# Sum of the routed experts: four gathered rows on TensorE and four on VectorE, LayerNorm's weight and bias on POOL

## The reference, cut to what is needed

```
def layer_norm(x, w, b):
    mu = jnp.mean(xf, -1, keepdims=True)
    var = jnp.mean(jnp.square(xf - mu), -1, keepdims=True)
    return ((xf - mu) * lax.rsqrt(var + EPS) * w + b)

# moe_ffn: acc[token] += (expert(token) @ w2[e]) * gate     for the 8 experts of the token
# shared = (silu(tf @ sw1) * (tf @ sw3)) @ sw2;  return acc + shared
f_all = moe_ffn(...)
h = layer_norm(DEEPNORM_ALPHA * h + mod[5] * f_all, ln_w[l, 1], ln_b[l, 1])
```

## Time and profile before

| | us |
|---|---|
| median of 3 runs | 2299.19 |
| lowest and highest | 2291.56, 2300.64 |
| the profiled execution | 2297.83 |
| its span | 2296.0 |
| TensorE busy | 1926.3 (84%) |
| VectorE busy | 854.0 (37%) |
| POOL busy | 652.5 (28%) |
| ScalarE busy | 261.1 (11%) |

### The profile page before, as it was taken

The page is one execution under the profiler, slowest core; times in us unless marked ns, Lnnn a source line. Parts: engine busy times, 40 slices in busy tenths (PEclk is TensorE's granted clock), DMA queues, the critical chain, the costliest instruction groups (busy, mean ns, idle before and its releaser), DMA issues. The chain is left out here.

```text
span 2296.0 us, 31832 instructions
## 1 busy us (share of the span) xinstructions
PE 1926.3 (84%) x10720; PEld 995.3 (43%) x10721; DVE 854.0 (37%) x1780; ACT 261.1 (11%) x541; POOL 652.5 (28%) x947
## 2 busy tenths in 40 slices
PE   6999994478789979999997878597779888877894
PEld 2334442344645544555553343244455444433442
DVE  0224446854533322333332736543343222222224
ACT  2122223211100000000001110011100000000001
POOL 0000000000156645666663000000046544444440
PEclk8999997789799999999998979798789999999998
DMA  8565510020759999989993761312199999999934
GB/s 347 205 239 205 193 37 1 1 97 0 298 210 409 411 415 413 397 320 406 389 411 116 311 249 55 130 53 97 67 368 408 412 413 413 413 412 411 409 139 201
DMA packets 99830, 601.66 MB, mean 262 GB/s; under 512 B 23232, under 2 KB 23339, under 8 KB 40300
## 3 DMA queue, kind: packets, MB, share of 16 engines
q1 hardware_dynamic: 64540, 499.67, 53.7%
q0 software_dynamic: 35216, 100.98, 11.7%
HBM read 590.50 MB, written 51.92 MB: 280 GB/s over the span
## 5 line engine op out<-in xcount | busy, mean ns | idle before, releaser
L1682 PE MATMUL bank<-moe_w,blk_xT 128*64 128x256 f32 x5632 | 684.5, 398 | 3.0 <-DVE blk_xT L1758 3.0
L1682 PEld LDWEIGHTS bank<-moe_w,blk_xT 128*64 128x64 f32 x5632 | 406.7, 143 | 223.8 <-issue 38.2
L1693 PE MATMUL bank<-moe_w,xt 128*64 128x512 f32 x1408 | 332.1, 592 | 1.5 <-DVE xt L1770 1.5
L1609 POOL DMA_INDIRECT ada_rows<-v_tokens,blk_gidx x264 | 271.7, 1029 | 140.3 <-issue 135.2
L1758 DVE STREAM_TRANSPOSE blk_xT<-ada_rows 128x512 f32<-128x512 f32 x132 | 94.0, 712 | 456.3 <-PE bank L1682 433.0
L435 PE MATMUL bank<-w_in_ring,xt 128*128 128x512 f32 x544 | 246.2, 610 | 12.6 <-DMA w_in_ring<-in_odd_w_in 9.8
L1625 POOL DMA_INDIRECT y_rows<-xt,blk_sidx x176 | 179.4, 1019 | 96.9 <-issue 48.5
L1777 DVE COPY xt<-bank 128x512 f32<-128x512 f32 x176 | 121.6, 691 | 149.3 <-PE bank L1693 149.3
L1741 ACT ACTIVATE xt<-bank 128x128 f32<-128x128 f32 x174 | 48.3, 278 | 1059.8 <-PE bank L1682 1059.8
L435 PEld LDWEIGHTS bank<-w_in_ring,xt 128*128 128x128 f32 x544 | 104.1, 195 | 148.4 <-issue 137.3
L1693 PEld LDWEIGHTS bank<-moe_w,xt 128*64 128x64 f32 x1408 | 100.9, 137 | 127.5 <-issue 100.5
(11 more groups left out here) (391 smaller groups left out, 1660.7 us busy)
## 6 DMA issues: line engine op xcount, KB each, us to landing
moe_w<-in_experts SPq DMA_DIRECT2D x128, 3072.0 KB, 32.2
even_late<-in_ada_w POOLq DMA_DIRECT2D x20, 2048.0 KB, 8.1
moe_w<-y_rows SPq DMA_DIRECT2D x24, 1024.0 KB, 20.5
w_in_ring<-in_even_w_in SPq DMA_DIRECT2D x8, 2048.0 KB, 9.0
w_in_ring<-in_odd_w_in SPq DMA_DIRECT2D x7, 2048.0 KB, 13.9
ada_ring<-in_ada_w SPq DMA_DIRECT2D x4, 2048.0 KB, 7.7
ada_rows<-v_tokens,blk_gidx POOLq DMA_INDIRECT x264
w_out<-in_even_w_out SPq DMA_DIRECT2D x1, 4096.0 KB, 12.9
```

The costliest lines, as they stand in the source:

```text
L1609: pool.indirect_dma_start(came[q][:, u], None, v_quarters, bass.IndirectOffsetOnAxis(ap=gidx[q][:, u:u + 1], axis=0), bounds_check=4 * n_t ...
L1682: last = nc.tensor.matmul(g.bank[1][64 * h:64 * h + 64, 0:HID], xT[:, k], w[:, s, (2 * k + h) * HID:(2 * k + h + 1) * HID], start=k == 0, ...
L1693: last = nc.tensor.matmul(g.bank[3][64 * h:64 * h + 64, :], hT[:, 64 * m:64 * m + 64], w[:, s, at:at + 512], start=m == 0, stop=m == 1)
```

## The change

`BY_PE` goes from 5 to 4, so rows 0 to 3 are TensorE's and rows 4 to 7 VectorE's. Each transfer of two rows then has one reader. `finish` leaves VectorE: the two operations are issued by POOL, with the semaphores `ln_weighted` between them and `ln_finished` behind them. Since `z` has two halves, VectorE waits before gathering tile n (n >= 2) until POOL has finished tile n - 2. And VectorE's `scale` of tile n comes directly behind its gathering, with no `finish` between them. In the mLSTM norm the scratch `sq` becomes the first half of `g.mod_row`'s first row, which holds nothing at that time.

```diff
--- before.py
+++ after.py
@@ -520,7 +520,7 @@
 
         self.e, self.y = sb("mlstm_e", [P, 2, NT, T]), sb("mlstm_y", [P, 2, NT, P])
         self.sm, self.negsel = sb("mlstm_small", [P, 2, 3, NT]), sb("negsel", [HEADS, HEADS, P])
-        self.sq, self.st, self.w = sb("mlstm_sq", [P, NT, P]), sb("mlstm_st", [P, 2, NT]), g.ada_rows[:, 0]
+        self.sq, self.st, self.w = g.mod_row[:, 0, 0:512].rearrange("p (n c) -> p n c", n=NT), sb("mlstm_st", [P, 2, NT]), g.ada_rows[:, 0]
         self.side_loaded, self.scored, self.rows_made, self.clamped, self.exped, self.weighted, self.read, self.summed = (new_sem(g, x) for x in (
             "mlstm_w_loaded", "scores_ready", "max_rows_ready", "clamped", "exp_ready", "weights_ready", "values_used", "values_summed"))
         self.mstep, self.var_ready, self.rooted, self.normed, self.mix_turned, self.mix_copied = (new_sem(g, x) for x in (
@@ -774,8 +774,8 @@
         link(nc.vector.tensor_reduce(st[:, 0], y, AX.X, ALU.add))
         link(nc.vector.tensor_scalar(st[:, 0], st[:, 0], 1.0 / P, None, ALU.mult))
         link(nc.vector.tensor_tensor(y, y, st[:, 0].unsqueeze(2).broadcast_to([P, NT, P]), ALU.subtract))
-        link(nc.vector.tensor_tensor(self.sq[:], y, y, ALU.mult))
-        link(nc.vector.tensor_reduce(st[:, 1], self.sq[:], AX.X, ALU.add))
+        link(nc.vector.tensor_tensor(self.sq, y, y, ALU.mult))
+        link(nc.vector.tensor_reduce(st[:, 1], self.sq, AX.X, ALU.add))
         nc.vector.tensor_scalar(st[:, 1], st[:, 1], 1.0 / P, EPS, ALU.mult, ALU.add).then_inc(self.var_ready, 1)
 
     def norm_scale(self, dve, h):
@@ -1166,9 +1166,9 @@
 
     nc = g.nc
     nt = len(tiles)
-    (ln_loaded, step, rooted, normed, diag_made, rows_used, rows_added) = (new_sem(g, x) for x in (
-        "ln_loaded", "ln_step", "ln_root", "ln_normed", "diag_made", "y_rows_used", "y_rows_added"))
-    BY_PE = 5
+    (ln_loaded, step, rooted, normed, diag_made, rows_used, rows_added, weighted, finished) = (new_sem(g, x) for x in (
+        "ln_loaded", "ln_step", "ln_root", "ln_normed", "diag_made", "y_rows_used", "y_rows_added", "ln_weighted", "ln_finished"))
+    BY_PE = 4
     BY_DVE = TOPK - BY_PE
     PAIRS = TOPK // 2
     RING = 13
@@ -1228,6 +1228,8 @@
                 def gather_up(n):
                     i, zz = tiles[n], z[:, n % 2]
                     v = 1 if i < 2 else 0
+                    if n >= 2:
+                        dve.wait_ge(finished, n - 1)
                     for k in range(BY_PE, TOPK):
                         at, count = piece(n, k)
                         dve.wait_ge(fetched[at], count)
@@ -1255,20 +1257,20 @@
                     link(nc.vector.scalar_tensor_tensor(mv[:, n, 3:4], mv[:, n, 0:1], -1.0, mv[:, n, 2:3], ALU.mult, ALU.mult))
                     marks["scale", n] = link.n
 
-                def finish(n):
-                    zz = z[:, n % 2]
-                    dve.wait_ge(normed, n + 1)
-                    if n == 0:
-                        dve.wait_ge(ln_loaded, 16)
-                    link(nc.vector.tensor_tensor(zz, zz, ln[:, 0], ALU.mult))
-                    link(nc.vector.tensor_tensor(g.h[:, tiles[n]], zz, ln[:, 1], ALU.add))
-
                 for n in range(nt):
                     gather_up(n)
-                    if n:
-                        finish(n - 1)
                     scale(n)
-                finish(nt - 1)
+
+            @block.gpsimd
+            def _(pool):
+                pool.wait_ge(ln_loaded, 16)
+                for n in range(nt):
+                    zz = z[:, n % 2]
+                    pool.wait_ge(normed, n + 1)
+                    pool.tensor_tensor(zz, zz, ln[:, 0], ALU.mult).then_inc(weighted, 1)
+                    pool.wait_ge(weighted, n + 1)
+                    pool.tensor_tensor(g.h[:, tiles[n]], zz, ln[:, 1], ALU.add).then_inc(finished, 1)
+                pool.wait_ge(finished, nt)
 
             @block.scalar
             def _(act):
```

## The result

The changed kernel takes 2309.41 us (median of 7 runs, 2302.83 to 2313.07), the kernel before 2293.63 us in runs beside it (2291.56 to 2300.64). The ratio of the two sets of runs (whose medians are 15.8 us apart and whose means 13.0) is 1.0055, with a 95% interval of 1.004 to 1.0069: 12.6 us slower, 9 to 16. The forecast was 0.57%, 13.0 us.

A forecast was written before the change was run, and what follows sets the result against it. VectorE was taken to bound the stage, balanced with TensorE within 0.2 us. Undisturbed -1.2 us plus collisions +14.2 gave +13.0 us, 2312.2 us against the 2299.19 median (0.57% slower), range 2303 to 2319.

The forecast's parts named there:

- TensorE's row: One gathered row less on TensorE: 1.7 us less a tile, 10.3 us needed, giving nothing by itself since VectorE is longer.
- VectorE's row: One multiply-and-add more on VectorE: 1.32 us a tile, hidden in tile 0 by the wait for the next transfer.
- The undisturbed tile: VectorE's tile without POOL's disturbance, two products fewer and one row more: 11.29 us against 12.19.
- POOL's product alone: One 1024-column product on POOL without a partner: 2.34 us, the middle between 2.17 and 2.52.
- The tail: End of the stage's last tile, ScalarE's scaling then two POOL products with nothing beside them: 6.1 us, against 3.86 before.
- Where the products fall: POOL's two products stop VectorE's third and fourth row of the next tile; the new wait before gathering costs nothing.
- The price of a collision: Each POOL product stopping a VectorE row costs 1.8 us, two a tile, four tiles: +14.2 us (13 to 18).
- TensorE's clock: TensorE's longer pause before the next stage costs nothing, since that stage already starts at a granted 0.50.
- The rival in which the whole product stands in VectorE's way: Each POOL product costs VectorE all its 2.34 us: 18.7 in place of 14.2, sum +17.5, 2317 us; chance 0.08.
- The rival without collisions: POOL's products overlap VectorE freely or fall beside PSUM reads or statistics: -1.2 us, 2298; chance 0.11.
- the one with a single collision: The second product gets in behind the fourth row, beside L1243 with its PSUM operand: +5.9 us, 2305; chance 0.07.
- the slow POOL: POOL's products are themselves slow, 4.0 us at 1024 columns, lengthening tails and collisions: 2332 us; chance 0.05.

The follow-up runs named there:

- the kernel with four rows each: The kernel before with BY_PE = 4 and nothing else, weight and bias still on VectorE: 56.11 and 29.09 us in the two stages, ratio 1.0009 to before.
- the kernel with POOL's fills: The changed kernel with POOL's product and sum replaced by two fills that read nothing: stages of 48.9 and 26.3 us, one execution, no ratio.
- the half-width kernel: The changed kernel with POOL's two operations on 512 of the 1024 columns: stages of 54.85 and 28.7 us, one execution, no ratio.
- the kernel with two steps and four rows: The kernel before with BY_PE = 4, ScalarE's scaling and VectorE's two products made two VectorE scalar-and-tensor steps: 54.15 and 27.28 us, ratio 1.0012.
- the last kernel: The kernel before with two VectorE scalar-and-tensor steps, five rows on TensorE, and LayerNorm's weight and bias transferred behind the fourth transfer of rows: ratio 0.9962 to before.
- the kernel with five and three rows: The changed kernel with BY_PE = 5, so three rows on VectorE, weight and bias on POOL: 55.75 and 32.50 us, ratio 1.0032 to before.

## Why the prediction was right

The forecast was +13.0 us, 1.0057; measured are 1.0055 by time and +14.1 us by the two stages. The mechanism held: what POOL's products cost, where they fall and the tail are shown by the rows and by the experiments. One price was too small. That 1.0057 and 1.0055 lie so close is in part luck, since the interval of the ratio is 3 us to either side, wider than the error of that price.

- *TensorE's row*: right in its size, 10.30 us a tile, and no wait of VectorE for TensorE is left. But that it gives nothing by itself, and that VectorE hardly rested from 1286.41 on, was read wrongly: VectorE waited 1.30 us for TensorE at 1291.11 and 0.78 in layer 1, and both waits are gone. The sum doesn't use that statement: it starts at the end of tile 0 and adds undisturbed tiles.
- *VectorE's row*: right. 1.32 us, free in tile 0; shown apart by the kernel with four rows each, +2.8 us, which is 5.3 less the two waits and the transfer.
- *The undisturbed tile* of 11.29 us: right. It is what the kernel with POOL's fills shows, 1299.35 to 1310.64.
- *POOL's product alone*: 2.34 us, as taken. That this was exact is partly luck: it was the middle between bounds of 2.17 and 2.52, and the start that doesn't grow is 0.18 us, not the 0.35 that I read.
- *The tail*: right, 6.1 us in both layers.
- *Where the products fall*: right. Rows three and four of the next tile, two collisions a tile, and VectorE's wait for `finished` never shows.
- *The price of a collision*: mis-sized. The step said 1.98 us of hold less 0.18, 1.8 us; measured are 2.18 us of hold (2287.20 to 2289.38) and 1.97 us lost. (Eight times 1.8 is moreover 14.4 and not the 14.2 that the sum has, and 13 to 18 less 1.2 gives bounds of 12 to 17, not 11 to 16.) The 0.35 us of start came from the product of the earlier trace rows that ended 0.91 us after VectorE; that product has a broadcast operand, and the 1.26 us from which it was subtracted are another line's, L1543. The plain 512-column one of the half-width kernel ends 1.13 us after the row ahead of it (1294.81 + 1.28 = 1296.09, and 1295.34 + 1.88 = 1297.22), so only 0.13 of its 1.26 us passes beforehand. With 1.97 the term is 15.8 and the sum -1.2 + 15.8 = 14.6, and less the 0.4 us of layer 1's earlier transfer it is the 14.1 of the traces.
- *TensorE's clock*: nothing, as said; the next stage's transposes take 6.20 us against 6.06, and that stage starts at a granted 0.50 in both (1341 to 1345 us here). In the kernel with two steps and four rows the same transposes take 5.59 us behind a pause of 22.4 us, and in the last kernel 6.34 behind 10.5, so the longer pause is not what sets them.
- *The scratch*: nothing, as said. The square takes 692 ns and the reduction 686 ns in both kernels.

The rival in which the whole product stands in VectorE's way was to give +17.5. The measured hold is 2.18 us of the product's 2.34, and VectorE's own start passes under it, so 1.97 is lost: the hold is a little nearer to the whole product than to my 1.98, the loss is nearer to my 1.8 than to 2.34, and so is the sum of 14.6.

The Trainium skill's page "SBUF — State Buffer" (section "SBUF: two separate sides") has the one that starts first hold the port for the whole instruction. The trace agrees but for 0.16 us of the product's 2.34, which pass while VectorE's earlier row still runs.

The rival without collisions is out by the undisturbed fills and the stopped rows; the one with a single collision describes the kernel with five and three rows, where the second product has the PSUM addition beside it; and the slow POOL is out by the last tile's 2.34 us.

The case's own noise deserves a word: medians of before moved from 2299.19 (3 runs) to between 2293.6 and 2296.3 (7 runs and more), so the ratio is what the forecast should be held to. The time of 2312.2 is 2.8 us above the measured one; the same 13.0 us on the later median would have been 2306.6, 2.8 below. And 0.5% is not what a measurement of this kernel can tell from no change, as the prediction has it: the intervals of the ratios reach 0.12 to 0.25% to either side.

## What to carry to other kernels

Work moved to an idle engine is free only if it doesn't stop the busy one. Here each POOL product of 2.34 us that read SBUF stopped a VectorE step with two operands in SBUF for 1.97 us, while POOL's fills (3.93 us for the three rows) and VectorE's additions from PSUM (1.41 us) passed. Small steps with one operand in SBUF were stopped too, 1.19 us in place of 0.20; the first row's step L1238, a wide one of that kind, never had a product beside it. Before moving a step, look in the trace for any place where both engines already run together and compare the durations with those of the same instruction alone. And price the tail apart from the steady state: a slower engine at the end of a stage costs its full difference, here 6.1 us against 3.86, and steps that fold a scalar and a tensor operation into one shorten just that end.

## What was not expected of the hardware

A late transfer changes who goes first. In the kernel with five and three rows a wait of 0.84 us for data let POOL's product in ahead of VectorE's row, and the two rows took 6.50 us in place of 4.57. So the cost of sharing can vary from tile to tile with transfers that have nothing to do with POOL. And the POOL product L1540, whose second operand is broadcast, ended 0.91 us after VectorE's step at 512 columns, a plain one of that width in the half-width kernel 1.13 us after. Whether the broadcast is the reason no run shows: L1540 never runs without a partner here, and L1543, which has a broadcast operand too, takes the 1.26 us of the plain one. The two should not be priced from each other.
